# One-hot placing matmuls of 128 columns: a token's high and low weights accumulated in PSUM

## The reference

```
sc = einsum('phcd,hcnd->phcn', q, sub_keys)          # 2 x 128 key scores for each head
top_s, top_i = top_k(sc, 16)
cand_s = top_s[:, :, 0, :, None] + top_s[:, :, 1, None, :]
cand_i = top_i[:, :, 0, :, None] * 128 + top_i[:, :, 1, None, :]
best_s, best_pos = top_k(cand_s, 16); idx = take(cand_i, best_pos)
g = softmax(best_s)
act = gelu(einsum('phkd,pd->phk', expert_u[idx], x))
out = einsum('phk,phkd->pd', g * act, expert_v[idx])
```

## Time and profile before

| what | value |
| --- | --- |
| median of three runs | 2233.41 us (2231.43 to 2236.27) |
| the profiled execution | 2236.16 us |
| its span in the profile | 2234.8 us |
| TensorE busy | 2153.6 us (96%), 11336 matmuls |
| VectorE, ScalarE, GpSimd busy | 1620.2, 1005.9, 952.7 us |
| HBM traffic | 433.31 MB read, 57.28 MB written |

### The profile page before, as it was taken

The page is one execution under the profiler, slowest core; times in us unless marked ns, Lnnn a source line. Parts: engine busy times, 40 slices in busy tenths (PEclk is TensorE's granted clock), DMA queues, the critical chain, the costliest instruction groups (busy, mean ns, idle before and its releaser), DMA issues.

```text
span 2234.8 us, 30577 instructions
## 1 busy us (share of the span) xinstructions
PE 2153.6 (96%) x11336; PEld 1950.2 (87%) x11336; DVE 1620.2 (72%) x2857; ACT 1005.9 (45%) x1878; POOL 952.7 (43%) x635
## 2 busy tenths in 40 slices
PE   6999999999999999999999999999999899999998
PEld 3777899999999999999999999988877688888887
DVE  6774579988897897999999999858565475344323
ACT  4433434577777774333333333544554433223221
POOL 0435336777733224656666676443423321111000
PEclk9999999999999999999999999999999999999999
DMA  8646236777779999999999999634242433333332
GB/s 307 194 136 229 92 100 175 202 188 191 196 202 325 346 328 360 375 411 407 410 410 410 407 410 407 213 101 143 72 113 68 147 122 95 96 102 95 100 94 81
DMA packets 195803, 494.96 MB, mean 221 GB/s; under 512 B 33084, under 2 KB 84412, under 8 KB 194944
## 3 DMA queue, kind: packets, MB, share of 16 engines
q1 hardware_dynamic: 131720, 311.51, 41.7%
q0 software_dynamic: 63936, 181.50, 23.1%
HBM read 433.31 MB, written 57.28 MB: 220 GB/s over the span
## 4 chain that ended last, share of the span: by engine, by line
PE 44%; DVE 14%; DMA 10%; issue 3%; ACT 1%; POOL 0%; DVEq 0%; ACTq 0%
PE bank L573 11%; PE bank L577 11%; PE bank L574 11%; DMA scores<-in_rows_v,row_at 6%; DVE scores L2097 4%; DMA scores<-in_rows_u,row_at 3%; DVE scores L2091 3%; DVE weights_lo L1673 3%; DVE hidden L2142 2%; PE bank_stat L949 1%; PE bank_stat L950 1%; PE bank_stat L954 1%; PE bank L994 1%; PE bank L981 1%; PE bank L979 1%
## 5 line engine op out<-in xcount | busy, mean ns | idle before, releaser
L573 PE MATMUL bank<-h_lo,weights_hi 128*128 128x384 f32 (+1 forms) x2148 | 769.8, 358 | 19.4 <-ACT h_hi L1422 7.1
L574 PE MATMUL bank<-h_hi,weights_hi 128*128 128x384 f32 (+1 forms) x2148 | 763.9, 356 | 0.0
L1133 ACT ACTIVATE weights_hi<-weights_raw 128x1024 fp32r<-128x1024 f32 (+1 forms) x411 | 431.8, 1051 | 319.2 <-DMA weights_raw<-in_expert_v 208.7
L1673 DVE TENSOR_TENSOR weights_lo<-weights_raw,weights_hi 128x1024 fp32r<-128x1024 f32 x347 | 438.7, 1265 | 101.3 <-ACT weights_hi L1133 98.7
L577 PE MATMUL bank<-h_hi,weights_lo 128*128 128x384 f32 (+1 forms) x2148 | 458.9, 354 | 0.7 <-DVE weights_lo L1673 0.7
L573 PEld LDWEIGHTS bank<-h_lo,weights_hi 128*128 128x128 f32 x2148 | 407.3, 190 | 55.6 <-ACT h_hi L1422 8.8
L574 PEld LDWEIGHTS bank<-h_hi,weights_hi 128*128 128x128 f32 x2148 | 407.3, 190 | 28.8 <-issue 0.2
L577 PEld LDWEIGHTS bank<-h_hi,weights_lo 128*128 128x128 f32 x2148 | 386.7, 188 | 30.1 <-DVE weights_lo L1673 1.0
L2534 POOL DMA_INDIRECT scores<-in_rows_u,row_at x128 | 171.4, 1339 | 242.1 <-DVE row_coef L2091 188.0
L2484 POOL TENSOR_TENSOR weights_lo<-weights_raw,weights_hi 128x1024 fp32r<-128x1024 f32 x64 | 160.1, 2506 | 238.6 <-ACT weights_hi L1133 238.5
L2547 POOL DMA_INDIRECT expert_coefs<-square x128 | 221.3, 1729 | 91.5 <-issue 45.4
(11 more groups left out here) (461 smaller groups left out, 3343.4 us busy)
## 6 DMA issues: line engine op xcount, KB each, us to landing
weights_raw<-in_expert_u SPq DMA_DIRECT2D x128, 512.0 KB
weights_raw<-in_expert_v SPq DMA_DIRECT2D x128, 512.0 KB
weight<-expert_coefs POOLq DMA_DIRECT2D x32, 768.0 KB
hidden_store<-hidden SPq DMA_DIRECT2D x28, 768.0 KB
hidden<-hidden_store POOLq DMA_DIRECT2D x28, 768.0 KB
expert_coefs<-stage SPq DMA_DIRECT2D x16, 1024.0 KB
ada_raw<-in_w_ada SPq DMA_DIRECT2D x26, 512.0 KB, 6.5
weights_raw<-in_w_ffn_gate SPq DMA_DIRECT2D x22, 512.0 KB
```

The costliest lines, as they stand in the source:

```text
L573: M.matmul(bank[:, 0:width], hi[:, c:c + P], m_lo[k][:, 0:width], start=start and i == 0, stop=False)
L574: M.matmul(bank[:, 0:width], hi[:, c:c + P], m_hi[k][:, 0:width], start=False, stop=False)
L1133: S.activation(w_hi[n % SPLIT][:, 0:w], w_raw[n % RAW][:, 0:w], ACT.Copy).then_inc(*hi_done.inc(n))
L1673: V.tensor_tensor(w_lo[n % SPLIT][:, 0:w], w_raw[n % RAW][:, 0:w], w_hi[n % SPLIT][:, 0:w].bitcast(F32), ALU.subtract).then_inc(*lo_dve.in ...
```

## The change

For each token the matmul of 256 columns becomes two of 128 columns, with the high weights and then the low ones, which are added in PSUM in the same 128 columns (start on the first, stop on the second). So a quad fills one bank, with four tables. ScalarE copies the whole bank to `stage` with one operation, and its copy is what frees the bank. VectorE's addition is gone. SyncE's store stands two steps behind the quad, waits for ScalarE, and so is issued two steps earlier than before.

```
-        def placed_at(tb, quad, half):
-
-            t0 = 4 * quad + 2 * half
-            return stage[(tb * P + t0) // TOK % 2][:, :, :, t0 % TOK:t0 % TOK + 2].rearrange("p g j t -> p (g j) t")
-
-        def placed_part(tb, quad, half, part):
-            return banks["place", tb, quad, half][:].rearrange("p (t h n) -> p h n t", t=2, h=2)[:, part]
+        def placed_at(tb, quad):
+
+            t0 = 4 * quad
+            return stage[(tb * P + t0) // TOK % 2][:, :, :, t0 % TOK:t0 % TOK + 4].rearrange("p g j t -> p (g j) t")
...
             def place(tb, quad):
                 M.wait_ge(*act["hot_weight", tb, quad])
                 tokens, weights = hot[quad % N_HOT][:, 0], hot_weight[quad % N_HOT]
-                for half in range(2):
-                    bank = take(("place", tb, quad, half))
-                    for t in range(2):
-                        ins = M.matmul(bank[:, 256 * t:256 * t + 256], tokens[:, 2 * half + t, :],
-                                       weights[:, 2 * half + t, :, :].rearrange("p h n -> p (h n)"), start=True, stop=True)
-                    ins.then_inc(*pe.inc(("place", tb, quad, half)))
-                pe.also(("place", (tb, quad)), ("place", tb, quad, 1))
+                bank = take(("place", tb, quad))
+                for t in range(4):
+                    for part in range(2):
+                        ins = M.matmul(bank[:, t * P:(t + 1) * P], tokens[:, t, :], weights[:, t, part, :],
+                                       start=part == 0, stop=part == 1)
+                ins.then_inc(*pe.inc(("place", tb, quad)))
...
-                for half in range(2):
-                    S.wait_ge(*pe["place", tb, quad, half])
-                    S.activation(placed_at(tb, quad, half), placed_part(tb, quad, half, 0), ACT.Copy) \
-                        .then_inc(*act.inc(("placed", tb, quad, half)))
+                S.wait_ge(*pe["place", tb, quad])
+                S.activation(placed_at(tb, quad), banks["place", tb, quad][:].rearrange("p (t n) -> p n t", t=4), ACT.Copy) \
+                    .then_inc(*act.inc(("place", tb, quad)))
...
-            def placed_quad(tb, quad):
-
-                for half in range(2):
-                    V.wait_ge(*act["placed", tb, quad, half])
-                    at = placed_at(tb, quad, half)
-                    V.tensor_tensor(at, placed_part(tb, quad, half, 1), at, ALU.add).then_inc(*dve.inc(("place", tb, quad, half)))
...
-                for tb, quad in HOT_AT.get(j - 3, ()):
-                    placed_quad(tb, quad)
...
             def store_stage(tb, quad):
                 s = (tb * P + 4 * quad) // TOK
-                Y.wait_ge(*dve["place", tb, quad, 1])
+                Y.wait_ge(*act["place", tb, quad])
...
             for j in range(AHEAD * GROUP):
-                for tb, quad in HOT_AT.get(j - 4, ()):
+                for tb, quad in HOT_AT.get(j - 2, ()):
                     if 4 * quad % TOK == TOK - 4:
                         store_stage(tb, quad)
```

More of the change, by code:

```diff
@@ L1385, in weigh_hot @@
                 if (tb, quad) in TWO_BEFORE:
-                    S.wait_ge(*pe["place", TWO_BEFORE[tb, quad]])
+                    S.wait_ge(*pe[("place", *TWO_BEFORE[tb, quad])])
                 for t in range(4):
@@ L2046, in make_hot @@
                 if (tb, quad) in TWO_BEFORE:
-                    V.wait_ge(*pe["place", TWO_BEFORE[tb, quad]])
+                    V.wait_ge(*pe[("place", *TWO_BEFORE[tb, quad])])
                 V.tensor_tensor(hot[quad % N_HOT][:], placed[:, 0:2, t0:t0 + 4].unsqueeze(3).broadcast_to([P, 2, 4, P]),
```

## The result

The changed kernel takes 2240.71 us (median of 7 runs, 2236.34 to 2243.27) against 2231.43 us (7 runs beside them). The ratio is 1.0039, with a 95% interval of 1.0027 to 1.0051: 9.3 us slower. In a second comparison it took 2237.84 us (8 runs) against 2232.24 (19 runs), a ratio of 1.0028 [1.0017, 1.0038], 5.6 us slower. The forecast was +11 us and 2244.5, with a range from 2237 to 2254: right in sign and mechanism, but too high. The first comparison lies 3.8 us under it; in the second the rise is only half of the forecast, and the time lies 0.8 us inside the lower end of the range.

A forecast was written before the change was run, and what follows sets the result against it. TensorE was taken to set the pace in the placing stretch; 28.5 - 13.3 - 2.7 - 1.6 = +10.9 us on the profiled 2236.16 us gave 2247, or 2244.5 us against the median, with a range of 2237 to 2254.

The forecast's parts named there:

- The matmuls: TensorE's placing: eight weight loads a quad take 0.92 us where four need 0.47, +28.5 us for 64 quads.
- The waits for `stage`: TensorE's bank waits for VectorE's addition in the placing stretch go, with their restarts: -13.3 us.
- The half clocks: Two stretches of TensorE at 1.2 GHz after stalls in the placing stretch go with the stalls: -2.7 us.
- ScalarE's waits: TensorE's waits for `hot_weight` while placing: two of three, 0.8 us each, go; the 2.4 us one stays: -1.6 us.
- restarts: TensorE's refill after each of nine bank stalls while placing, 0.27 us each: 2.4 us that go.
- VectorE's time: 128 additions, 48.2 us busy, leave VectorE in the placing stretch; worth nothing beyond the waits already counted.
- The store: SyncE's store of `stage`, issued two steps earlier: later weight loads are covered and its earlier end gains nothing.
- The mix starts later and runs as before: The expert mix after placing starts later by what TensorE lost and takes as long as before.
- Cheap matmuls: Rival at each quad's eight matmuls: loads skipped or hidden, 0 to 11 us added, so 2216 to 2227; chance 0.11.
- A wait that moves to `hot_weight`: Rival: TensorE waits for `hot_weight` at the same heavy placing steps, +20 to +28.5, 2253 to 2262; chance 0.09.
- More half clocks: Rival: 1.2 GHz stretches come more often, 1.35 us each, four more give 2250; chance counted within the forecast's 0.80.

The follow-up runs named there:

- e2: The kernel before with each 256-column placing matmul split into two of 128 to separate columns, VectorE's additions kept: 2249.97 us, ratio 1.008.
- e3: The kernel before without VectorE's additions (low parts left out), ScalarE's copy freeing the bank, store at two steps: 2217.38 us, ratio 0.9934.
- e4: The changed kernel with only each token's high matmul, four of 128 columns a quad (low parts left out): 2215.36 us, ratio 0.992.
- e1: The kernel before with VectorE's additions and the store of `stage` one step earlier: 2216.21 us, ratio 0.9926.
- e5: The changed kernel with VectorE making each quad's `hot` twice: 2238.07 us, against 2237.84 for the change in the same round.
- e7: The changed kernel with the store of `stage` back at four steps behind the quad: 2239.00 us.
- e8: The kernel before with VectorE's additions two steps earlier, in the step of ScalarE's copy: 2234.17 us, ratio 1.0009.

## Why the prediction was right

- **The matmuls, +28.5 us.** Right in kind, a little too large: 0.92 us for eight against 0.47 for four, by the chain's distance of 5.08 against 4.63, in the change and in e2. e3 and e4 show the reason, the load. (0.45 x 64 is 28.8; the forecast writes 28.5.) The steady part of the stretch grew from 388.2 to 415.1, by 26.9 us, since the typical addition is 0.43 and not 0.45. By the Trainium skill's (TensorE: Matmul & The Clock Gate, Back-to-back issue gap) 81 ns a matmul, eight would take an estimated 0.65 us. This case's traces do not agree: 0.92 us were measured, 0.115 each, with float32r operands.
- **The waits for `stage`, -13.3 us.** Right: none is left in the change, and e1 removes them with the additions in place.
- **The half clocks, -2.7 us.** The two windows went from 0.98 to 1.00, as said. No run separates them from the stalls.
- **ScalarE's waits, -1.6 us of 3.9.** This term was sized too small. I kept the wait of 2.4 us that came from a late weight transfer. It went too: `hot_weight` is waited for 0.6 us in all, so 3.3 us went and not 1.6. In the faster kernels e1 and e3 it is still 3.1 and 3.2 us, in e2 0.7, and in e4, with ScalarE's single copy but four matmuls, 4.3. So what removed it is the slower pace of TensorE and not the single copy, of the two reasons that the forecast gave.
- **The miss in the stretch.** It grew by 6.4 us and not by 10.9. Outside the steady part it had 23.1 us of waits, restarts and slow clock before and has 2.6 after: 20.5 went, where the forecast had 17.6. So of the 4.5 us, 1.6 are the matmuls (26.9 for 28.5) and 1.7 ScalarE's waits. The last 1.2 are restarts, half clocks and small gaps, 6.3 where the forecast had 2.4 + 2.7 = 5.1; no run divides these. All three terms missed the same way.
- **VectorE's time, nothing.** Right, by e5. **The store, nothing.** Right, by e7.
- **The mix starts later and runs as before.** Right: 339.30 us busy in its window against 339.27, and VectorE's first product with a coefficient starts at 870.4 us against 866.2.
- **The rivals.** Cheap matmuls fell with e2 and e4; the change itself has 0.92 us a quad, where this rival needed less than 0.75. A wait that moves to `hot_weight` did not come in the change; e8 shows that it is a real case in this kernel, at another place of the addition. More half clocks did not come in the stretch.
- **The sum.** +10.9 forecast, +9.3 and +5.6 measured in two rounds. That the first comparison came within 2 us of the forecast is in part luck: the stretch grew by 6.4 us only, and the changed kernel's two medians lie 2.9 us apart. What is explained of the miss is the part in the stretch.

## What to carry to other kernels

Count weight loads, not columns, where the matmuls are this narrow (with 384 columns one already took 0.173 us, more than the 0.112 between two loads): splitting a matmul of 256 columns into two of 128 with the same stationary operand doubled its cost here, and an addition in PSUM that needs one more load must be paid by the engine that sets the pace. When that engine waits for a bank, look at where the releasing operation stands in its engine's order before taking the operation away: one step earlier gave 16.8 us for nothing, and two steps earlier gave nothing.

## What the runs showed of the hardware that was not expected

A slower TensorE hides the lateness of others to a degree that changes the balance. Splitting the matmuls alone (e2) put 26.9 us on the busiest engine and lengthened the stretch by 14.3 (17.0 in the median), because waits, restarts and half clocks of 12.6 us went with the slower pace. Two matmuls into the same columns, the second adding, ran at the same distance as two into separate ones (5.08 us from quad to quad and a steady part of 415.1 us in both). And the changed kernel's medians in two rounds differed by 2.9 us (2240.71 and 2237.84) while its stretch was 417.7 us in both.
